# Plain float32 products in attention and recurrence, and weight tiles in two transfers

## The reference, cut to what matters

```
h = concat(meta, x)
h = h + mla(rms_norm(h));    h = h + peer(rms_norm(h), layer 0)
h = h + rglru(rms_norm(h));  h = h + peer(rms_norm(h), layer 1)
out = rms_norm(h)[:, 16:]

mla:   a = h @ w_in (1024 -> 704);  q = norm(a_q) @ w_q_up;  kv = norm(a_kv) @ w_kv_up
       8 heads: softmax(q k^T * scale, causal) @ v;  o @ w_out (1024 -> 1024)
rglru: proj = h @ w_in (1024 -> 2048); xc = conv4(proj right half); gate = gelu(left half)
       r, i = sigmoid(xc @ gate matrices); a = exp(-8 r softplus(-lam)); b = sqrt(1 - a^2) * i * xc
       hs[t] = a[t] hs[t-1] + b[t];  (hs * gate) @ w_out
peer:  q = h @ w_query (1024 -> 2048); top 16 of 16384 experts per head by product keys
       sum over experts of  softmax gate * gelu(u_e . h) * v_e
```

## Time and profile before

| | |
|---|---|
| median of 3 runs | 1746.57 us (1742.76 to 1748.43) |
| the profiled execution's own time | 1746.25 us |
| its span, first to last instruction | 1744.5 us |
| mean granted TensorE clock | 0.988 |
| PE busy | 1653.8 us (95%) |
| PE weight loads busy | 1550.5 us (89%) |
| DVE busy | 1147.7 us (66%) |
| POOL busy | 631.6 us (36%) |
| ACT busy | 278.8 us (16%) |
| DMA | 533.94 MB in 149917 packets, mean 306 GB/s |

### The profile page before, as it was taken

The page is one execution under the profiler, slowest core; times in us unless marked ns, Lnnn a source line. Parts: engine busy times, 40 slices in busy tenths (PEclk is TensorE's granted clock), DMA queues, the critical chain, the costliest instruction groups (busy, mean ns, idle before and its releaser), DMA issues. The chain is left out here.

```text
span 1744.5 us, 35217 instructions
## 1 busy us (share of the span) xinstructions
PE 1653.8 (95%) x12806; PEld 1550.5 (89%) x12806; DVE 1147.7 (66%) x2449; ACT 278.8 (16%) x752; POOL 631.6 (36%) x538
## 2 busy tenths in 40 slices
PE   8999999999999999999888999989999999999998
PEld 7858899888999998888778888988899999989897
DVE  4562369984699896545648823999458999944442
ACT  4553221111110000000025621211111100000000
POOL 5614011353244445333416621033433444533310
PEclk9999999999999999999899999999999999999999
DMA  4303477999999999999963235799999999999984
GB/s 155 133 13 102 133 265 270 364 381 366 344 408 403 389 398 408 410 409 410 394 241 112 97 125 178 258 349 354 392 336 354 408 391 395 409 405 403 383 341 157
DMA packets 149917, 533.94 MB, mean 306 GB/s; under 512 B 17617, under 2 KB 20434, under 8 KB 149842
## 3 DMA queue, kind: packets, MB, share of 16 engines
q1 hardware_dynamic: 89938, 314.90, 48.3%
q0 software_dynamic: 59904, 218.13, 32.4%
HBM read 531.92 MB, written 1.05 MB: 306 GB/s over the span
## 5 line engine op out<-in xcount | busy, mean ns | idle before, releaser
L308 PE MATMUL ps<-big,raw 128*128 128x160 f32 (+2 forms) x4608 | 701.3, 311 | 22.7 <-DMA raw<-in_u 16.9
L308 PEld LDWEIGHTS ps<-big,raw 128*128 128x128 f32 x4608 | 656.1, 190 | 55.5 <-issue 20.8
L1313 PE MATMUL ps<-big,raw 128*128 (+1 forms) x4096 | 600.9, 304 | 21.9 <-DMA raw<-in_v_rows 8.7
L1313 PEld LDWEIGHTS ps<-big,raw 128*128 128x128 f32 x4096 | 563.9, 191 | 49.6 <-issue 46.0
L1356 POOL DMA_INDIRECT big<-in_u_rows,big x208 | 252.8, 1215 | 589.4 <-DVE big L1482 414.6
L1499 DVE SCALAR_TENSOR_TENSOR big<-big 128x1024 f32<-128x1024 f32 x201 | 258.1, 1284 | 202.3 <-PE ps L1313 127.5
L1356 POOL DMA_INDIRECT big<-in_v_rows,big x208 | 225.8, 1086 | 314.2 <-DVE big L1499 255.9
L1482 DVE CUSTOM_DVE_ANT_0 big<-big 128x1024 f32<-128x1024 f32 x208 | 244.5, 1224 | 10.1 <-DMA big<-in_u_rows,big 10.1
L265 POOL TENSOR_TENSOR wlo<-raw,whi 128x512 fp32r<-128x512 f32 x98 | 136.6, 1411 | 94.5 <-ACT whi L259 94.1
L1396 ACT ACTIVATE big<-ps 128x160 f32 x256 | 77.6, 303 | 545.4 <-PE ps L308 510.7
L393 ACT ACTIVATE big<-h 128x272 f32<-128x272 f32 (+1 forms) x32 | 12.6, 418 | 585.5 <-DVE h L1573 575.2
(11 more groups left out here) (184 smaller groups left out, 1143.1 us busy)
## 6 DMA issues: line engine op xcount, KB each, us to landing
raw<-in_u SPq DMA_DIRECT2D x256, 512.0 KB
raw<-in_v_rows SPq DMA_DIRECT2D x256, 512.0 KB
raw<-in_query SPq DMA_DIRECT2D x32, 512.0 KB, 3.3
raw<-in_lru_w SPq DMA_DIRECT2D x24, 512.0 KB, 3.2
raw<-in_mla_down SPq DMA_DIRECT2D x17, 512.0 KB, 3.4
raw<-in_mla_out SPq DMA_DIRECT2D x8, 512.0 KB, 3.3
big<-in_u_rows,big POOLq DMA_INDIRECT x208
big<-in_v_rows,big POOLq DMA_INDIRECT x208
```

The source lines that it names most:

```text
L308: mm = pe.matmul(out, self.mem.raw[:, s, c * P:(c + 1) * P], x[:, c, :], start=(c == 0), stop=(c == DC - 1))
L1313: return pe.matmul(accumulator(c), mem.raw[:, s, c * P:(c + 1) * P], act_w[:, i, :], start=start, stop=False, skip_group_check=True)
```

## The change

Three things change together.

1. `Stream.multiply`, the class `Cut` and all cutting go; the attention and recurrent stages call `multiply_raw` on float32 as the expert layers do. POOL has no work left in MLA and RG-LRU. The dummy products become 14 in place of 26 ahead of the two first tiles, and the 24, 40 and 86 others are gone.
2. Each weight tile is loaded by two transfers of 256 KB (2 KB in each partition), each with its own semaphore; PE waits for each half, and SP reloads each half when PE has used it. This holds for all stages, but the four tiles that a stage loads ahead for the next one remain single transfers.
3. In RG-LRU the first convolution moves ahead of the softplus chain.

```diff
-        self.landed = [sem(f"landed{s}") for s in range(UNROLL)]
+        self.landed = [sem(f"landed{q}") for q in range(HALVES)]
+    def load_half(self, sp, s, src, e):
+        sp.dma_start(self.mem.raw[:, s, e * HW:(e + 1) * HW], src[:, e * HW:(e + 1) * HW]).then_inc(self.landed[2 * s + e], 16)
     def load_read(self, sp, turn, s, src):
-        sp.wait_ge(self.done, (turn - 1) * HALVES + 2 * (s + 1))
-        sp.dma_start(self.mem.raw[:, s, :], src).then_inc(self.landed[s], 16)
+        for e in range(2):
+            sp.wait_ge(self.done, (turn - 1) * HALVES + (2 * s + e + 1))
+            self.load_half(sp, s, src, e)
+    def wait_half(self, pe, turn, s, e):
+        pe.wait_ge(self.landed[2 * s + e], turn * 16 + 16)
     def multiply_raw(self, pe, turn, s, out, x, scaled=None):
-        pe.wait_ge(self.landed[s], turn * 16 + 16)
         pe.wait_ge(self.free[s % 2], turn * 2 + (s // 2 + 1))
         for c in range(DC):
+            if c % (DC // 2) == 0:
+                self.wait_half(pe, turn, s, c // (DC // 2))
...
@@ -632,8 +503,6 @@
-                act.wait_ge(o_out, head + 1)
-                act.copy(mem.xhi[:, at_head, :], o[:, at_head, :]).then_inc(out_cut.hi_cut, 1)
...
@@ -772,52 +629,49 @@
-            keep_busy(pe, mem, 6, 26)
+            keep_busy(pe, mem, 6, 14)
             for n in range(n_down):
-                down.multiply(pe, n // UNROLL, n % UNROLL, down.bank(n), cut if n == 0 else None)
+                down.multiply_raw(pe, n // UNROLL, n % UNROLL, down.bank(n), xn, norm.scaled if n == 0 else None)
...
-            keep_busy(pe, mem, 6, 24)
...
-            multiply_turns(pe, proj, 0, DC // UNROLL, out_cut)
+            for s in range(UNROLL):
+                proj.multiply_raw(pe, 0, s, proj.bank(s), o, o_out if s == 0 else None)
+            with pe.Fori(1, DC // UNROLL) as turn:
+                for s in range(UNROLL):
+                    proj.multiply_raw(pe, turn, s, proj.bank(s), o)
...
@@ -1055,25 +841,7 @@
-            scale_and_cut(dve, norm, xn, cut)
...
+            norm.scale(dve, xn)
...
+            convolve(0)
+            dve.wait_ge(lam_exp, 1)
...
-            ycut.lo(dve, 0)
...
@@ -1112,21 +898,19 @@
-            keep_busy(pe, mem, 6, 26)
+            keep_busy(pe, mem, 6, 14)
             for n in range(2 * DC):
-                st.multiply(pe, n // UNROLL, n % UNROLL, st.bank(n), cut if n == 0 else None)
+                st.multiply_raw(pe, n // UNROLL, n % UNROLL, st.bank(n), xn, norm.scaled if n == 0 else None)
-                    keep_busy(pe, mem, 6, 40)
-            keep_busy(pe, mem, 6, 86)
-            multiply_turns(pe, st, OUT, END, ycut)
+            for s in range(UNROLL):
+                st.multiply_raw(pe, OUT, s, st.bank(s), b, states if s == 0 else None)
...
@@ -1315,8 +1102,9 @@
-        pe.wait_ge(st.landed[s], turn * 16 + 16)
         for c in range(DC):
+            if c % (DC // 2) == 0:
+                st.wait_half(pe, turn, s, c // (DC // 2))
```

More of the change, by code:

```diff
@@ L240, in load_ahead @@
             sp.dma_start(self.mem.raw[:, s, :], tiles[s]).then_inc(self.mem.ahead[s], 16)
     def loaded_before(self, sp, times):
-        for landed, ahead in zip(self.landed, self.mem.ahead):
+        for s, ahead in enumerate(self.mem.ahead):
             sp.wait_ge(ahead, 16 * times)
[L246 to L267, removed]
+            for e in range(2):
+                sp.sem_inc(self.landed[2 * s + e], 16)
     def open(self, pe):
@@ L411, in add @@
                   skip_group_check=True)
[L414 to L441, removed]
 def mla(nc, ctx, mem, d):
@@ L579, in _ @@
             norm.root(act)
-            first_cuts(act, down, norm, cut)
             act.wait_ge(reduced, 1)
@@ new lines, in half_of @@
+            def half_of(k):
+                n, e = (2 * n_down + k) // 2, k % 2
+                down.wait_half(pe, n // UNROLL, n % UNROLL, e)
+                return mem.raw[:, n % UNROLL, e * HW:(e + 1) * HW]
+            for k, blocks_of in enumerate(halves):
+                w = half_of(k)
+                for b, (m, c) in enumerate(blocks_of):
+                    first, last = c in (0, QC), c in (QC - 1, QC + KVC - 1)
+                    if first:
+                        latent_ready(m)
+                    mm = pe.matmul(mem.ps[:, 4 + m % 4, 0:L], w[:, b * P:(b + 1) * P], latn[:, c, :], start=first,
+                                   stop=last)
+                mm.then_inc(down.done, 1)
@@ L820, in _ @@
-                passes(todo, 2 * n_down + k)
+                    if c == 0:
+                        latent_ready(m)
+                    mm = pe.matmul(mem.ps[0:rows, 4 + m % 4, :], latn[:, QC + c, t * P:t * P + rows], w,
+                                   start=(c == 0), stop=(c == KVC - 1))
+                mm.then_inc(down.done, 1)
             pe.wait_ge(down.free[0], (n_down + 1) // 2 + 1)
@@ L893, in update_residual @@
     next_sum.gather(dve, DC - 1)
-def first_los(pool, stream, cut):
-    for e in range(2):
-        stream.cut_lo(pool, 0, 0, e)
-        for c in (e * DC // 2 + 1, e * DC // 2 + 3):
-            cut.lo_chunk(pool, c)
-def lo_of_turns(pool, stream, turns, cut):
-    first_los(pool, stream, cut)
-    for s in range(1, UNROLL):
-        for e in range(2):
-            stream.cut_lo(pool, 0, s, e)
-    if turns > 1:
-        with pool.Fori(1, turns) as turn:
-            for s in range(UNROLL):
-                for e in range(2):
-                    stream.cut_lo(pool, turn, s, e)
-def multiply_turns(pe, stream, first, last, cut):
-    for s in range(UNROLL):
-        stream.multiply(pe, first, s, stream.bank(s), cut if s == 0 else None)
-    with pe.Fori(first + 1, last) as turn:
-        for s in range(UNROLL):
-            stream.multiply(pe, turn, s, stream.bank(s))
 def tile_of(tiles, turn, s):
@@ L1000, in _ @@
             norm.root(act)
-            first_cuts(act, st, norm, cut)
             act.wait_ge(lam_abs, 1)
@@ L1137, in _ @@
                               stop=True).then_inc(gated, 1)
-            keep_busy(pe, mem, 6, 86)
-            multiply_turns(pe, st, OUT, END, ycut)
+            for s in range(UNROLL):
+                st.multiply_raw(pe, OUT, s, st.bank(s), b, states if s == 0 else None)
+            with pe.Fori(OUT + 1, END) as turn:
+                for s in range(UNROLL):
+                    st.multiply_raw(pe, turn, s, st.bank(s), b)
             keep_busy(pe, mem, 6, 14)
@@ L1675, in _ @@
             for s in range(UNROLL // 2, UNROLL):
-                pe.wait_ge(st.landed[s], END * 16)
+                for e in range(2):
+                    st.wait_half(pe, END - 1, s, e)
             for c in range(DC):
```

224 lines of the change are left out of this document (44 added, 180 removed).

## The result

The changed kernel takes 1765.25 us (median of 4 runs, 1759.44 to 1776.42); beside it the kernel before took 1747.5 (1742.76 to 1754.72, 4 runs). The ratio is 1.0101, with a 95% interval of 1.0068 to 1.0134: about 1% slower. The forecast was 1739.8, in a range of 1724 to 1764, with 0.25 for slower. The profiled execution was the shortest of the four: 1759.44 us (span 1757.7), 13.2 more than that of before.

The account below looks back on a forecast made before the run. The prediction took PE and the chains around it to bound 280 us and the DMA 1400 us. From the profiled 1746.25 us it took -10.5 for attention and recurrence and +4 for two transfers, giving 1739.8, range 1724 to 1764.

Parts of the forecast that it names:

- +4: Weight loads: net cost in us taken for 2 KB packets, a third of the upper end less 2 us of earlier data.
- upper end: Weight loads: 5.1% on weights for one more packet start, 2.6% on the mix, 18 us over 700 us of full slices.
- B: Rival, expert layers: weights fall to one third while gathers queue, 3.84 us per tile, +22; 1761.8, up to 1783; chance 0.18.
- first half: Attention and recurrence, plain float32 without cuts: MLA +7.4 and RG-LRU -17.9, together -10.5 us.
- D: Rival, weight loads: 2 KB loads pay the whole 18 us and nothing is gained, 1753.8 us; chance 0.10.
- (a): MLA start: fewer fillers, PE starts at 15.2 and is through eight tiles and the norm sums at 46.9 us.
- (c): MLA up blocks: 64 plain blocks at 0.458 are 29.3 us against 24.2 for 16 half tiles, +5.1 us.
- (d): MLA: 12 value products of 512 columns take 10.3 us; +1.3 up to +2.6, taken as +2 us.
- (e): MLA heads: ACT's cast (0.42 us) is free for six heads and in the chain for the last two, -0.8 us.
- (f): MLA output: eight plain float32 tiles at 0.65 us more each, +5.2 us.
- A: Rival, weight loads: finer data pays, no DMA cost shows and half tiles bring 8 us, 1727.8 us; chance 0.18.
- C: Rival, RG-LRU: DVE stays slow without POOL or a chain holds PE, output 6 to 12 us late, 1746 to 1752; chance 0.06.

Follow-up runs that it names:

- twoq: Changed kernel, but in both expert layers' tails SP issues each tile's first half and ACT the second, packets still 2 KB; 1747.45 us, ratio 1.0055.
- whole_again: Changed kernel with weight tiles loaded whole again (512 KB, 4 KB packets, one semaphore), all else as changed; 1721.77 us, ratio 0.9913.
- lrupool: Changed kernel with whole tiles, plus 32 unused POOL subtractions of 128x512 float32 in RG-LRU; 1736.54 us, ratio 0.999.
- cast: Changed kernel with whole tiles, plus one more ACT copy of each head's output in MLA, where the cast was; 1721.89 us, ratio 0.9911.
- coarse: Changed kernel's two transfers of 2 KB packets, but asked for and awaited tile by tile; 1792.35 us, ratio 1.0325.
- lanes: Changed kernel with each tile's two transfers cut by partitions (64 each, 4 KB packets), asked for and awaited tile by tile; 2264.52 us, ratio 1.3018.

## Why the prediction was wrong

**The price of 2 KB packets: the step that failed.** "I take +4 (a third of the upper end, less 2 us of earlier data)." It is +36.4 us on top of the rest of the change, +32.8 alone. Two things were true together that the prediction kept apart as rivals.
- The rate. Its upper end (5.1% for each packet start, 2.6% on the mix, 18 us) was nearly right: 5.9 to 6.2%, and 2.7% on the mix, by which an estimate is 19 us over the same 700 us. I divided it by three because the 1 us window of the earlier trace rows "was still filling". Nothing in the rows asked for that. By the Trainium skill (DMA: Bandwidth & Descriptors, "Why small descriptors are slow") an estimate is 2.3% on the weights; these runs show more than twice that.
- The share. B had the mechanism and nearly its price (+22): equal numbers of packets from each queue, 3.84 us a tile while gathers are queued (3.9 measured). What is left of 36.4 beside 19 is 17, an estimate by difference; twoq measured about 12 of the share's cost, in the tails. The Trainium skill (the same page, "Queues, rings and completion order") says that an engine changes queue at packet boundaries only; the counts of 357 to 399 and 363 to 365 agree. B's sentence "the tail itself hardly changes" was wrong: I let the rows' schedule hold in the tail. But the gathers overtook the weights there, and 15.4 us of layer 0's 30.7 lie in it (260.3 against 244.9 in whole_again), 9.9 of them by the share. (These two traces are 44.6 us apart, more than the medians' 36.4, so the parts are somewhat large.) That B's 22 lies near 17 is in part luck, since it stood for the bursts alone. B's own sign did come: PE waits 30.1 us for u tiles in the kernel after, 16.9 before.

B was then priced at 1761.8 with the small +4 for the rate in it. With the rate's upper end it is 1775.8, and with the first half as it came out 1768.6 (1746.25 - 17.7 + 18 + 22), 9 above the profiled run. B and D excluded each other only in my list.

**The first half.** Forecast -10.5, measured -17.7 between the traces, -17.0 and -16.6 in the medians.
- RG-LRU was right by its own steps: -17.8, PE as the bound from tile 1 to the last one, 97.1 us from the fillers to the last update where "about 97" stood. lrupool shows the cause named, the contention on DVE, for 14.0 us of it, with the lower clock after each wait, which the prediction did not have.
- MLA was forecast at +7.4 and came out at +0.1. (a) There are seven down tiles and not eight, so PE was through at 43.0, 3.9 us earlier than forecast (a tile is 3.7); that was a miscount. (c) 64 blocks took 29.3 us, as forecast. (d) the value products end at 83.85: +2.4 against the up blocks for the +2 taken. (e) The heads gave 3.1 us in place of 0.8 (the output tiles began at 133.32 before and begin at 129.81), and (f) the output tiles cost 3.6 in place of 5.2, since the first of them ran at the lower clock before. None of the rows that I went by covers the clock of the last heads: 0.74 from 120 to 140 us before, as in cast, which shows the cause.

**Rivals.** A (finer data pays) is right in a way that does not help here: coarse shows 32 us for landing by halves where the packets had taken the share, and no run shows it with whole packets. C did not come in: DVE's small operations take 0.17 us and PE does not wait in RG-LRU. D's 18 us came in, and B's with them.

## What to carry to other kernels

Where two DMA queues are backlogged, count packets, not bytes: the queue with the smaller packets lost share in proportion, and here it did not regain it once the other queue had run dry. Before cutting a transfer for earlier data, look at what the cut does to the packets: by columns it halved them, and by partitions it kept them and cost far more (lanes). A second queue for the same stream gave the share back, and not the rate. And when two mechanisms have one trigger, their prices add: list them as terms, not as rivals.

## What was not expected of the hardware

- A tile moved as two transfers of 64 partitions each ran at 260 GB/s with the engines' share at 1.03, for 409 with all 128 partitions, and the gathers' packets beside it took 0.23 us in place of 0.146.
- DVE operations of 8 columns take 1.12 to 1.24 us if a subtraction of 128x512 float32 on POOL overlaps them, and 0.17 if not. In lrupool each of the five long ones ends within 0.05 us of the end of the subtraction beside it (913.25 + 1.24 against 913.06 + 1.39, for one). 32 such subtractions (1.3 to 1.6 us each) made a stage of 97 us 14 us longer.
- 0.55 us more of idle PE in front of a head's products was followed by the lower clock: 2.45 us for 1.35.
- One more packet start per 4 KB costs about the same at 2 KB and at 1 KB, 6.2 and 5.9% of the stream's time.
